# The low parts of 20 weight units move from VectorE to GpSimd, inside the attentions

## The reference

```
for i in range(2):                                  # first block
    z = rms_norm(x) @ w_in[i]
    o_a = mla_attention(...)    # 8 heads, every query block sees all 512 keys
    o_b = fourier_mix(h)
    o_c = windowed_gqa(...)     # 8 heads, at most 3 key blocks of 128, distance bias
    merged = sigmoid(g_a) * (o_a @ w_branch_a[i]) + sigmoid(g_b) * (...) + sigmoid(g_c) * (...)
    x = x + rms_norm(merged @ w_out[i]);  x = x + ffn(x);  x = x + gated embedding
# second block, one layer: recurrent branch, pooling branch, sparse attention (8 heads,
# the best 128 earlier keys), merge, attention over 256 memory rows (m @ w_mem_kv), ffn
```

## Time and profile before

| what | us |
|---|---|
| median of 3 runs | 3041.79 |
| lowest and highest run | 3031.34, 3041.89 |
| span of the profiled execution | 3034.1 |
| PE busy | 2869.4 (95%) |
| DVE busy | 1492.0 (49%) |
| ACT busy | 1071.6 (35%) |
| POOL busy | 449.6 (15%) |

### The profile page before, as it was taken

One profiled execution on the slowest core, in us unless ns is written; L12 is line 12 of the kernel. 1 busy time (PEld: TensorE's weight loads), 2 busy tenths in 40 slices (PEclk: granted clock), 3 DMA queues, 4 the chain that ended last, 5 costly groups with the idle time before them and its releaser, 6 DMA issues. The chain is left out here.

```text
span 3034.1 us, 34691 instructions
## 1 busy us (share of the span) xinstructions
PE 2869.4 (95%) x12356; PEld 2219.2 (73%) x12356; DVE 1492.0 (49%) x2199; ACT 1071.6 (35%) x1631; POOL 449.6 (15%) x283
## 2 busy tenths in 40 slices
PE   6999999899999899999989999989999998899998
PEld 4885567688887688556768888767676676578886
DVE  4346673543324534668444332445578734553333
ACT  4334432422223433443333222342533333432221
POOL 1010011311102301001131111230011113211101
PEclk9999999999999899999999999999998899999999
DMA  3221012222232222201222222222232122122232
GB/s 120 95 94 56 15 56 83 70 97 97 97 111 90 72 96 85 70 15 46 81 83 97 97 96 98 97 70 84 83 108 73 42 70 84 42 83 97 97 109 86
DMA packets 37046, 245.79 MB, mean 81 GB/s; under 512 B 4144, under 2 KB 5168, under 8 KB 7984
## 3 DMA queue, kind: packets, MB, share of 16 engines
q1 hardware_dynamic: 33600, 239.09, 23.1%
q10 hardware_dynamic: 3312, 4.93, 0.5%
HBM read 241.91 MB, written 2.10 MB: 80 GB/s over the span
## 5 line engine op out<-in xcount | busy, mean ns | idle before, releaser
L505 PE MATMUL bank<-h_hi,w_hi 128*128 128x512 f32 x2152 | 863.2, 401 | 39.9 <-DVE h_lo L1403 28.9
L506 PE MATMUL bank<-h_lo,w_hi 128*128 128x512 f32 x2152 | 844.6, 392 | 0.0
L507 PE MATMUL bank<-h_hi,w_lo 128*128 128x512 f32 x2152 | 844.6, 392 | 0.0
L1320 DVE TENSOR_TENSOR w_lo<-raw,w_hi 128x2048 fp32r<-128x2048 f32 x225 | 520.3, 2313 | 561.5 <-ACT w_hi L924 386.8
L505 PEld LDWEIGHTS bank<-h_hi,w_hi 128*128 128x128 f32 x2152 | 407.9, 190 | 148.6 <-issue 33.2
L507 PEld LDWEIGHTS bank<-h_hi,w_lo 128*128 128x128 f32 x2152 | 407.6, 189 | 86.6
L506 PEld LDWEIGHTS bank<-h_lo,w_hi 128*128 128x128 f32 x2152 | 408.1, 190 | 85.3 <-issue 4.3
L924 ACT ACTIVATE w_hi<-raw 128x2048 fp32r<-128x2048 f32 x137 | 261.8, 1911 | 313.5 <-PE bank L507 303.6
L507 PE MATMUL bank<-a_hi,w_lo 128*128 128x512 f32 x528 | 205.6, 389 | 0.0
L505 PE MATMUL bank<-a_hi,w_hi 128*128 128x512 f32 x528 | 205.6, 389 | 0.0
L506 PE MATMUL bank<-a_lo,w_hi 128*128 128x512 f32 x528 | 205.5, 389 | 0.0
(11 more groups left out here) (353 smaller groups left out, 3964.7 us busy)
## 6 DMA issues: line engine op xcount, KB each, us to landing
raw<-in_stream SPq DMA_DIRECT2D x226, 1024.0 KB, 4.9
x<-in_xT SPq DMA_DIRECT2D x2, 1024.0 KB, 11.8
out_T<-x ACTq DMA_DIRECT2D x8, 256.0 KB, 2.1
p_f<-in_pT ACTq DMA_DIRECT2D x2, 512.0 KB, 3.8
memf<-in_memT ACTq DMA_DIRECT2D x1, 1024.0 KB, 5.8
cst_sb<-in_cst ACTq DMA_DIRECT2D x1, 411.5 KB, 6.1
pos_i<-in_pos ACTq DMA_DIRECT2D x1, 258.0 KB, 8.8
vec<-in_vec ACTq DMA_DIRECT2D x2, 26.0 KB, 1.8
```

Of the source, the lines that this page charges most:

```text
L505: nc.tensor.matmul(ps, wh, xh, start=start, stop=False)
L506: nc.tensor.matmul(ps, wh, xl, start=False, stop=False)
L507: return nc.tensor.matmul(ps, wl, xh, start=False, stop=stop)
L1320: nc.vector.tensor_tensor(w_lo[s][:, :], raw[s][:, :], w_hi[s][:, :].bitcast(F32), ALU.subtract).then_inc(lo_ready, 1)
```

## The change

For the 20 units GpSimd now makes the low part too, right after the high part. VectorE's `split_unit` does nothing in the marked stages. As two engines now raise `lo_ready`, each makes sure that the earlier low parts are counted: GpSimd waits for its own high part and for the low part of the unit before, and VectorE, at the first unit of every other stage, for the units before it.

```
-                    dve.wait_ge(pool_hi_ready, c.at("HP", st, u + 1))
-                else:
-                    dve.wait_ge(hi_ready, c.own_units(st, u + 3))
+                    return
+                if u == 0:
+                    dve.wait_ge(lo_ready, c.at("U", st, 2))
+                dve.wait_ge(hi_ready, c.own_units(st, u + 3))
                 low_part(v % 2)
...
                     nc.gpsimd.tensor_tensor(w_hi[v % 2][:, :], raw[v % 2][:, :], ones[:, 0:1].to_broadcast([P, UC]), ALU.mult).then_inc(pool_hi_ready, 1)
+                    pool.wait_ge(pool_hi_ready, c.at("HP", st, u + 1))
+                    pool.wait_ge(lo_ready, c.at("U", st, u + 2))
+                    nc.gpsimd.tensor_tensor(w_lo[v % 2][:, :], raw[v % 2][:, :], w_hi[v % 2][:, :].bitcast(F32), ALU.subtract).then_inc(lo_ready, 1)
```

## The result

| | before | after |
|---|---|---|
| median of the runs, us | 3039.31 (4 runs, 3031.34 to 3041.89) | 3069.66 (4 runs, 3068.81 to 3075.53) |
| span of the profiled execution, us | 3034.1 | 3066.7 (its time 3068.81) |
| mean granted TensorE clock | 0.975 | 0.972 |

The changed kernel takes 1.0106 times as long, 95% interval 1.0088 to 1.0125. The change of the median is +30.4 us, that of the span +32.6. The forecast was 3073 with a range from 3050 to 3092, so the time lies inside, 3 us from the forecast.

A forecast was written before the change was run, and what follows sets the result against it. TensorE sets the pace, delayed only by VectorE coming late. Windowed 15.8, latent 2.0, sparse 8.4 and clock 3.4 and 2 sum to 31.6 us, added to the median of 3041.79: 3073 us, range 3050 to 3092.

The forecast's parts named there:

- removal of 20 low parts: VectorE loses 20 x 2.29 = 45.8 us of work, but it has slack, so the gain is 0.
- low part on GpSimd: Each of the 20 added GpSimd instructions of 128x2048 takes 4.6 us, between 4.5 and 5.2.
- its start behind the high part: GpSimd's low part starts about 0.2 us after the high part's end, by estimate.
- windowed pauses, one layer: Windowed attention: held scalings delay TensorE by 3.5, 1.1, 1.3, 1.0, 1.0 and 0 us at six units, 7.9 in all.
- windowed pauses, both: Windowed attention of two layers running the same program: TensorE delays of 15.8 us in all.
- windowed clock: TensorE's clock drops behind the 3.5 us pause of each layer's first windowed unit: 2 x 1.7 = 3.4 us.
- latent: Latent attention: at the second unit a held scaling moves the logits by 1.0 us; two layers, 2.0 us.
- sparse pauses: Sparse attention: scalings held behind the four low parts delay TensorE by 1.2, 2.1, 1.8 and 3.3 us, sum 8.4.
- sparse clock: Sparse attention: lower TensorE clock behind the longer pauses adds 2 us, bounds 0 and 5.
- The first rival: GpSimd's low part takes 5.2 instead of 4.6 us, 0.6 more at 16 units, +9.6: 3083 us; chance 0.15.
- the second rival: At windowed units VectorE's scaling starts before the low part and passes; total +15 us, 3057; chance 0.22.
- The third rival: Not slower: GpSimd's two-operand low part does not hold VectorE fully, no new TensorE wait; 3042 us, chance 0.12.

## Why the prediction was right, point by point

| term of the sum | predicted | measured |
|---|---|---|
| removal of 20 low parts | 0 | 0 (+1.9, interval -0.6 to +4.6, all of the change but the low part) |
| low part on GpSimd | 4.6 us | 4.54 |
| its start behind the high part | 0.2 | 0.16 windowed and latent, 0.08 sparse |
| windowed pauses, one layer | 3.5, 1.1, 1.3, 1.0, 1.0, 0 | 3.26, 0.98, 1.22, 0.88, 0.88, 0 |
| windowed pauses, both | 15.8 | 14.5 |
| windowed clock | 3.4 | 2.9 (-0.9 and +3.8) |
| latent | 2.0 | at most 1.3 |
| sparse pauses | 8.4 | 5.3 |
| sparse clock | 2 (0 to 5) | 7.2 |
| not in the sum: between layer 2's windowed stretch and the sparse one | 0 | 1.7 |
| sum | 31.6 | 32.9, of 32.6 in the span |

**How close the sum came.** Nearer than its terms. The two sparse terms were off by -3.1 and +5.2 us, and that they nearly cancel with the rest is luck; the windowed pauses, half of the sum, came out by their arithmetic.

**What bounds the kernel.** Right. TensorE sets the pace, VectorE's load doesn't matter, and what delays TensorE is VectorE coming late. The kernel without low parts shows the first half, the changed kernel the second. The 1.3 us of pauses that the prediction read in the windowed stretch of the earlier trace rows lie before its first logits: from the first logits to the last the kernel before has no idle time at all (116.15 of 116.15 us).

**What is held.** The prediction names the merge update on line 1642 as held beside GpSimd's high parts. The trace of before doesn't show that: none of the 16 updates lies beside one, and all take 0.69 us. After the change two of them lie beside a low part and take 4.44 us, so the statement came out true, but it had no row behind it.

**The low part.** Bounded between 4.5 and 5.2 from a 1024-column row and a 512-column row, taken at 4.6, and it took 4.50 to 4.56. The wider row was the one to trust: four pieces of 512 columns took 5.12 us at the unit looked at, 0.6 more than the one of 2048. The first rival falls with this. The Trainium skill (GPSIMD Engine Reference, "Elementwise — side-by-side cycle accounting") gives 4497 ns, and here the trace agrees with it.

**The windowed pauses.** Right to 0.25 us each. Half of the difference at the first unit is the low part: it ends 4.67 us behind the high part (358.19 to 362.86), where I had 4.8. The rest I leave.

**Which of the two comes first.** The forecast and the second rival differed in 0.05 us. In the trace the low part starts 0.09 us ahead of the scaling at both units shown. So the start was on the forecast's side; had it not been, the kernel with the wait shows +17 us instead of +30. This was the one step on which half of the result hung, and it could not have been decided from the rows of before. The Trainium skill (SBUF — State Buffer, "Who interferes with whom") says that the first to issue gets the ports for its whole instruction. The low parts of after agree with it, since they are ahead at both units, but they do not bear on the doubt: the earlier trace rows have a scaling ahead by 0.03 us and held all the same. What decides between starts this close stays open.

**The latent units.** Over-sized. The second unit of layer 1, of after:

```profile
280.12 4.51 POOL L1897 TENSOR_TENSOR w_lo<-raw,w_hi 128x2048 fp32r<-128x2048 f32 x1 [0.16 <-POOL w_hi L1894]
...
281.14 3.77 DVE L1482 TENSOR_SCALAR prob<-prob,st_rec 128x512 f32<-128x512 f32 x1
...
286.57 1.13 PE L632 MATMUL bank<-k_a,q_a 128*128 128x512 f32 x2 [0.54 <-ACT prob L1032]
```

The scaling ends 0.28 us behind the low part and the logits wait as forecast, but for 0.54 us where the forecast had them 1.0 later.

**The sparse attention.** Its total was under-sized, 10.4 for 12.4, and its two terms both wrong in size. The mechanism is the predicted one. The second unit:

```profile
2408.75 4.52 POOL L1897 TENSOR_TENSOR w_lo<-raw,w_hi 128x2048 fp32r<-128x2048 f32 x1
...
2409.25 0.74 PE L502 MATMUL bank<-w_hi,mem_hi 128*128 128x512 f32 x1
...
2410.29 3.26 DVE L1482 TENSOR_SCALAR prob<-prob,st_rec 128x512 f32<-128x512 f32 x1
...
2410.77 1.65 PE L632 MATMUL bank<-kk,qd 64*128 64x384 f32 x2
...
2413.61 1.11 PE L642 MATMUL bank<-cst_sb,prob 128*128 128x128 f32 x4 [1.20 <-DVE prob L1482]
```

The high part and the same matmuls of before, up to the one at 2389.06 in the earlier trace rows:

```profile
2382.42 3.60 POOL L1893 TENSOR_TENSOR w_hi<-raw,cst_sb 128x2048 fp32r<-128x2048 f32 x1 [21.85 <-PE bank L507]
...
2386.59 0.47 PE L502 MATMUL bank<-w_hi,mem_hi 128*128 128x512 f32 x1
...
2388.12 1.01 PE L632 MATMUL bank<-kk,qd 64*128 64x384 f32 x2 [0.59 <-ACT prob L1032]
```

The 512-column scaling is held to 0.28 us behind the low part's end. TensorE turns the tile 8.5 us behind the start of the high part (which starts at 2405.07), and did so 6.6 behind it before: +1.9 where I had +2.1. But as a pause only 0.6 of it shows (a pause of 1.20 in place of one of 0.59), since TensorE works at the lower clock on its way there: 0.74 us instead of 0.47 for the matmul on line 502, 1.65 instead of 1.01 for the logits. A pause that falls into slow work is shorter, but the slow work costs what the pause saves. The third unit reads the same, +1.6 for +1.8 and a pause of 1.11 in place of one of 0.59; the first has a new pause of 0.92 for +1.2. Only at the last unit the pause itself grew as predicted, from 0.67 to 3.89 (+3.2 for +3.3).

The step that failed is the clock term: "I add 2 for the longer pauses, bounds 0 and 5" had only the mean of the stretch, 0.79, behind it. The clock over 4 us at the second unit, of before, where a pause of 1.69 us ends at 2386.29 and the clock is 1.00 from 2384 to 2388:

```profile
2388.00:2392.00 4.00, 3.88 (x15) 2.91 (x16) 3.45 (x7) 1.85 (x6) 0.00 (x0) 0.60 0.00 0
2392.00:2396.00 4.00, 4.00 (x21) 2.60 (x20) 2.33 (x7) 0.95 (x3) 0.00 (x0) 0.97 0.64 207
```

and of after, where the same pause of 1.69 us ends at 2408.94:

```profile
2408.00:2412.00 4.00, 3.06 (x8) 1.58 (x8) 3.90 (x7) 1.14 (x4) 3.92 (x2) 0.66 0.00 0
2412.00:2416.00 4.00, 2.80 (x12) 2.06 (x12) 3.83 (x8) 1.08 (x3) 1.27 (x1) 0.50 0.35 96
2416.00:2420.00 4.00, 4.00 (x18) 3.46 (x17) 0.58 (x3) 0.71 (x2) 0.00 (x0) 0.56 0.40 168
```

Before, the clock falls 2 to 3 us behind the first pause, is at 1.2 GHz for some 3 us, and is full again. After, it is low within 1 us of the end of the like pause, the second pause (1.2 us, from 2412.4) lies in the low stretch, and the clock stays low for 10 us. The third unit shows both pictures again. In matching stretches of the two traces the second and the third unit have 2.6 us more busy time each, the first about 1.3 and the last 0.8. A second pause that lies in low clock went with a clock that stayed low; that it kept it low is not shown, and it can't be what lowered it, since the clock fell ahead of it. Why it fell sooner behind an equal pause stays open. The rows of before would have allowed a better guess: three of the four new pauses were known to lie some 4 us behind an old one, and the old one had already lowered the clock.

**The windowed clock.** Right in sum by luck. I had given each of the two 3.5 us pauses 1.7 us. The two came out at 3.26 us both, but in layer 1 the clock stayed at 1.00, and in layer 2 it fell to 0.68 and again to 0.74 (stretches of 5 us of after, the first in layer 1):

```profile
365.00:370.00 5.00, 5.00 (x23) 3.09 (x22) 4.62 (x17) 3.13 (x11) 0.00 (x0) 1.00 0.41 169
...
1365.00:1370.00 5.00, 5.00 (x17) 3.39 (x16) 3.98 (x17) 2.93 (x10) 0.00 (x0) 0.68 0.52 198
...
1410.00:1415.00 5.00, 5.00 (x25) 4.35 (x23) 4.09 (x14) 2.05 (x7) 0.00 (x0) 0.74 0.47 190
```

The same program on the same engine with the same pauses. What differs, I can't say; no run here was made for it. The traces of other kernels with this pause don't repeat the pattern in full: with only the windowed units on GpSimd the clock falls in layer 1 too (0.50 from 361 to 366), with the memsets only in layer 2. The second of layer 2's low stretches stands behind a pause of 1.22 us, which the prediction had given nothing. The trace of before could have warned: the earlier trace rows show 0.66 behind the 2.46 us pause at the end of layer 1's windowed attention, and behind the same pause in layer 2, which ends at 1451.85, there is no loss:

```profile
1452.00:1457.00 5.00, 5.00 (x45) 4.57 (x45) 3.38 (x3) 0.93 (x2) 0.00 (x0) 1.00 0.17 21
```

After the change this old pause costs clock in layer 2 as well (0.66 from 1470 to 1475). It lies in the 1.7 us that the sum didn't have, of which 1.4 are busy time over the same 3647 matmuls. So what a pause of 2.5 to 3.3 us costs in clock is a range that begins at nothing, and the prediction took one number from one place.

**The third rival.** Falls: two-operand instructions of GpSimd hold VectorE fully, for 4.57 us.

## What to carry to other kernels

In this kernel work given to GpSimd was not priced by the time it takes there or by what it frees elsewhere, but by how long one instruction of it holds VectorE's next instruction with two SBUF operands or wide scaling, and by who waits for that one; look for the engine that waits, not for the busy shares. A long GpSimd instruction beside VectorE's short ones is worth cutting: in four pieces the low part cost 2 us instead of 30, and the high part that had been there all along gave back 0.4 to 0.6%. And count a pause of TensorE with what it does to the clock, as a range and not as one number. When you compare a stretch of two traces, match it by its matmuls, and look at how the runs scatter before you take one profiled execution for all of them.

## What was not expected of the hardware

- Between GpSimd instructions that follow each other with nothing in between, VectorE's waiting instruction gets in: with four pieces of 1.03 to 1.48 us the 128x1 sum beside them took 0.24 to 0.78 us, where one instruction had held it for 1.1 to 3.3, and no scaling took more than 1.37.
- Pieces are not free: four instructions of 512 columns make a high part in 4.04 to 4.53 us where one of 2048 takes 3.60.
- A wait of GpSimd for its own instruction ahead costs 0.16 us, and 0.08 in the sparse attention's loop. A memset of 128x4 behind it starts 0.06 us before the recorded end of that instruction.
- Equal pauses of 3.26 us lowered TensorE's clock in layer 2 and not in layer 1, and equal ones of 2.46 us, before the change, in layer 1 and not in layer 2.
- The clock of the first sparse stretch returned to 2.4 GHz after 39 us in one trace and after 16 us in another, with the same work up to there; that is worth some 12 us.
